# A hybrid decoder step on one core: the mixer's tiles moved under its heads

## What is computed

```python
u = hn @ w_in                       # hn = rmsnorm(h); D_IN = 4640
xa, za, ia, fa, zb, xbc, dtr = split(u)
xc = silu(causal_conv(xa))          # 4 taps
q, k = xc @ w_q, xc @ w_k;  v = xa @ w_v      # per head, 8 heads of 128
h_a = mlstm(q, k, v, ia, fa)        # scores * decay, state C, n, m
h_a = rms(h_a) * norm_a * sigmoid(za)
xs, B, C = split(silu(causal_conv(xbc)))      # 16 heads of 64, state 128, 2 groups
y = ssd(xs, softplus(dtr), B, C) + d_skip * xs
y = group_rms(y * silu(zb)) * norm_b
h = h + concat(h_a, y) @ w_out
h = h + moe(rmsnorm(h))             # 16 experts, top-2 of a top-1 group
```

## Time and profile before

| | us |
|---|---|
| median of 3 runs (lowest, highest) | 933.55 (930.46, 938.48) |
| the profiled execution, its own time | 930.9 |
| its span, first to last instruction | 929.2 |
| PE, DVE, ACT, POOL busy | 830.6, 316.4, 149.8, 104.2 |
| mean granted TensorE clock | 0.955 of full |

### The profile page before, as it was taken

One profiled execution on the slowest core, in us unless ns is written; L12 is line 12 of the kernel. 1 busy time (PEld: TensorE's weight loads), 2 busy tenths in 40 slices (PEclk: granted clock), 3 DMA queues, 4 the chain that ended last, 5 costly groups with the idle time before them and its releaser, 6 DMA issues.

```text
span 929.2 us, 9631 instructions
## 1 busy us (share of the span) xinstructions
PE 830.6 (89%) x3774; PEld 443.0 (48%) x3774; DVE 316.4 (34%) x635; ACT 149.8 (16%) x368; POOL 104.2 (11%) x135
## 2 busy tenths in 40 slices
PE   5999999998587789999999899989899788999785
PEld 4888788665344458875332243322433223333221
DVE  3966601699978740043002012002111020020203
ACT  2222211543211220051110010100000100101002
POOL 5000000574644410000000000000000000000000
PEclk9999999998677779989999999999999999999999
DMA  8834333568565424930799999999999999999992
GB/s 241 269 113 159 134 115 136 159 194 247 155 183 161 130 84 183 358 115 1 303 409 410 409 409 410 409 409 409 409 409 409 409 409 410 409 409 410 409 409 105
DMA packets 110067, 263.01 MB, mean 283 GB/s; under 512 B 7127, under 2 KB 46219, under 8 KB 110009
## 3 DMA queue, kind: packets, MB, share of 16 engines
q1 hardware_dynamic: 107856, 257.94, 74.2%
q0 software_dynamic: 1648, 3.33, 1.2%
q10 hardware_dynamic: 520, 1.15, 0.4%
HBM read 251.66 MB, written 10.91 MB: 283 GB/s over the span
## 4 chain that ended last, share of the span: by engine, by line
PE 60%; DMA 14%; DVE 13%; SPq 8%; issue 2%; ACT 2%; ACTq 0%; DVEq 0%
PE bank L1421 13%; PE bank L1736 13%; DMA ring<-in_w_up 10%; PE bank L1788 8%; SPq L557 8%; PE bank L1638 6%; PE bank L1718 6%; DVE shared L1090 4%; PE bank L1751 3%; DMA ring<-in_w_down 2%; PE bank L1603 2%; DVE ring L1114 2%; DVE h_tok L1109 2%; PE bank L1560 1%; DVE YS L1118 1%
## 5 line engine op out<-in xcount | busy, mean ns | idle before, releaser
L1736 PE MATMUL bank<-ring,arena 128*64 128x512 f32 x1024 | 226.8, 594 | 26.4 <-DMA ring<-in_w_up 20.1
L1736 PEld LDWEIGHTS bank<-ring,arena 128*64 128x64 f32 x1024 | 73.3, 137 | 176.9 <-issue 131.6
L1421 PE MATMUL bank<-arena,ring 128*128 128x280 f32 x576 | 136.2, 399 | 0.8 <-ACT arena L797 0.8
L1788 PE MATMUL bank<-ring,arena 128*64 128x512 f32 x512 | 113.6, 595 | 14.6 <-ACT arena L942 14.2
L1421 PEld LDWEIGHTS bank<-arena,ring 128*128 128x128 f32 x576 | 109.4, 190 | 27.6 <-issue 1.2
L1355 DVE TENSOR_TENSOR arena<-bank,arena 128x512 f32<-128x512 f32 x16 | 11.1, 692 | 244.2 <-PE bank L1736 244.2
L1788 PEld LDWEIGHTS bank<-ring,arena 128*64 128x64 f32 x512 | 36.4, 137 | 81.6 <-issue 78.9
L1638 PE MATMUL bank<-arena,ring 128*128 128x264 f32 x256 | 59.6, 394 | 0.0
L434 DVE COPY arena<-bank 64x512 f32<-64x512 f32 x16 | 10.9, 683 | 137.9 <-PE bank L1788 137.9
L1718 PE MATMUL bank<-arena,xn 128*128 128x256 f32 (+1 forms) x192 | 54.2, 412 | 0.7 <-DVE arena L1327 0.7
L1638 PEld LDWEIGHTS bank<-arena,ring 128*128 128x128 f32 x256 | 49.5, 195 | 9.3 <-issue 0.7
(11 more groups left out here) (336 smaller groups left out, 749.2 us busy)
## 6 DMA issues: line engine op xcount, KB each, us to landing
ring<-in_w_gate SPq DMA_DIRECT2D x32, 2048.0 KB, 21.1
ring<-in_w_up SPq DMA_DIRECT2D x32, 2048.0 KB, 23.5
ring<-in_w_down SPq DMA_DIRECT2D x32, 2048.0 KB, 19.8
ring<-in_w_in SPq DMA_DIRECT2D x9, 2048.0 KB, 8.7
ring<-in_w_out SPq DMA_DIRECT2D x4, 2048.0 KB, 8.0
out<-h_tok SPq DMA_DIRECT2D x16, 512.0 KB, 3.5
h_tok<-in_state_ssm SPq DMA_DIRECT2D x8, 512.0 KB, 5.2
h_tok<-in_state_mlstm_C SPq DMA_DIRECT2D x8, 512.0 KB, 5.2
```

Source lines behind the costliest of these rows:

```text
L1421: last = mm(bank[n % 4][:, 0:T], slot_k(u % MR, 512)[:, k, o:o + P], hT[:, k, :], start=(k == 0), stop=(k == KD - 1))
L1736: last = mm(b[CAP * half:CAP * (half + 1), :], XG[:, k, e * CAP:(e + 1) * CAP], w[:, kk, half * 512:(half + 1) * 512], start=(k == 0), sto ...
L1788: last = mm(bank[5][CAP * half:CAP * (half + 1), :], HT[:, kk, u * CAP:(u + 1) * CAP], w[:, kk, half * 512:(half + 1) * 512], start=(u == ...
```

## The change

The mixer is put in another order, the arithmetic is the same up to rounding and these identities: silu(y) = (tanh(y/2) + 1) * y/2, with conv weights and biases halved beforehand (V_CAW to V_NB and from V_CBB); sigmoid likewise; 1/sqrt by Sqrt and a VectorE reciprocal in place of Ln and Exp.

- TensorE: after the 8 xa tiles and the tables the mLSTM heads begin. The x/B/C tiles stand inside them, two in each of heads 0 to 3, one in each of heads 4 to 7; the z tiles, zb first, stand ahead of the SSD heads, one each. All these 28 tiles use one PSUM bank, 5 (`b5_free`). The output projection begins before the last scales are done, and has no scales stage ahead of it: heads' scales are broadcast inside the SSD heads and inside the projection.
- The C states go by head and not by sample: a block holds one head's C of all 8 samples; it is decayed, updated and read in that head. The read is eight calls with a single weight column, one per sample, to partitions 0, 32, 64, 96 of banks 0 and 1, summed by two more calls. The SSD states go into the SSD heads, one sample in two heads.
- V of the samples goes to DRAM and back per head (`v_rows`).
- The decay products of the states and XWT move from GpSimd to ScalarE (eight, or six, activations with a scale by partition); the first convolution step, with the bias, moves from VectorE to ScalarE; the k of the samples is copied and weighted by VectorE. GpSimd only issues DMAs and copies a column per head.
- The scores of SSD heads are multiplied straight from PSUM (`GT` is gone).
- Weight blocks: order xa, qkv, x/B/C, zb, za, w_out, with an explicit list of slots. The first three expert blocks are requested before the last w_out block.

The core of the diff:

```diff
-WIN = [O_XA, O_XA + 512, O_XBC, O_XBC + 512, O_XBC + 1024, O_ZA, O_ZA + 512, O_ZB, O_ZB + 512]
-U_QKV = len(WIN)
+WIN = [O_XA, O_XA + 512, None, O_XBC, O_XBC + 512, O_XBC + 1024, O_ZB, O_ZB + 512, O_ZA, O_ZA + 512]
+U_QKV = WIN.index(None)
...
+UNIT_SLOT = [0, 1, 2, 0, 1, 0, 1, 2, 0, 1, 2, 0, 1, 2]
...
+XBC_A, XBC_B = [0, 2, 4, 6, 8, 9, 10, 11], [1, 3, 5, 7]
```

On SP:

```diff
+            def v_rows(h):
+
+                sp.wait_ge(s.v_sb, h + 1)
+                sp.dma_start(v_dram[h].rearrange("(b e) -> b e", e=P), VS[:, h * P:(h + 1) * P]).then_inc(s.rows_out, 16)
+                sp.wait_ge(s.rows_out, 32 + 16 * (h + 1))
+                if h >= 2:
+                    sp.wait_ge(s.st_new, h - 1)
+                sp.dma_start(VB[h % 2], v_dram[h:h + 1, :].to_broadcast([P, NB * DH])).then_inc(vb_in[h % 2], 16)
...
+            v_rows(0)
+            for h in range(HA):
+                row_load(h + 4)
+                if h + 1 < HA:
+                    v_rows(h + 1)
+                state_step(h)
...
+            expert_unit(0, 0, s.y_ps, HB)
+            expert_unit(0, 1, s.yb_norm, KD)
+            expert_unit(0, 2, s.yb_norm, KD)
+            mixer_unit(U_OUT + 3)
```

On ScalarE:

```diff
+            def decay_state(n):
+
+                act.wait_ge(st_in[n % 3], 16 * (n // 3 + 1))
...
+                for j in range(NB):
+                    w = BCM[:, n, j:j + 1] if n < HA else XE[:, j, n - HA:n - HA + 1]
+                    part = state_buf(n)[:, j, :]
+                    last = a.activation(part, part, ACT.Copy, scale=w)
+                last.then_inc(s.st_dec, 1)
...
+            for h in range(HA):
+                first_tap(3 + 2 * h)
+                first_tap(4 + 2 * h)
+                tanh_of_conv(2 + 2 * h)
                 if h + 1 < HA:
                     head_in(h + 1)
+                decay_exp(h + 1)
+                tanh_of_conv(3 + 2 * h)
+                decay_state(h + 1)
+                evac(HA + XBC_A[h])
...
+                cq_copy(h)
                 head_out(h)
+                if h < 4:
+                    evac(HA + XBC_B[h])
+                if h == 4:
+                    lct_copy(2, bank[5], s.b5_free)
...
+            for h in range(HB):
+                if h + 1 < HB:
+                    decay_exp(HA + h + 1)
+                if h % 2 == 0:
+                    weighted_x(h // 2)
+                elif h + 1 < HB:
+                    decay_state(HA + h // 2 + 1)
+                z_tanh(h)
+                if h % 2 == 0 and h >= 2:
+                    y_square(h // 2 - 1)
+                if h == 3:
+                    a.preload_act_table(ACT.Sqrt)
```

On VectorE, in the mLSTM heads:

```diff
+                c_update(h)
+                conv_taps(3 + 2 * h)
+                if h + 1 < HA:
+                    sample_q_k(h + 1)
+                conv_gate(2 + 2 * h)
+                conv_taps(4 + 2 * h)
+                conv_gate(3 + 2 * h)
```

On VectorE, in the SSD heads:

```diff
+                c = h // 2
+                dve.wait_ge(s.gt_ps, h // (HB // NG) + 1)
+                weighted(HA + h, bank[3 + h // (HB // NG)])
                 if h + 1 < HB:
                     ssd_args(h + 1)
+                if h == 1:
+                    denominators()
+                if h == 4:
+                    head_scales()
                 if h % 2 == 0 and h >= 2:
+                    ssd_out(dve, c - 1)
+                    gate_y(c - 1)
+                    s_read(c - 1)
+                if h % 2 == 1:
+                    s_update(c)
+                if h < KD:
+                    dve.wait_ge(s.z_sig, h + 1)
+                    v.scalar_tensor_tensor(out=ZB[:, h, :], in0=ZB[:, h, :], scalar=1.0, in1=bank[5][:, 0:T],
+                                           op0=ALU.add, op1=ALU.mult).then_inc(s.b5_free, 1)
+                if h % 2 == 1 and h >= 9:
+                    num_out((h - 9) // 2)
```

On TensorE:

```diff
+            def c_read(h):
+
+                pe.wait_ge(s.st_new, h + 1)
...
+                for b in range(NB):
+                    j = b % 4
+                    last = mm(bank[b // 4][32 * j:32 * j + 1, QT:QT + P], QS[:, h, b:b + 1], state_buf(h)[:, b, :],
+                              start=True, stop=True, skip_group_check=True)
+                last.then_inc(s.cq_ps, 1)
...
                 if h + 1 < HA:
                     head_proj(h + 1)
+                if h >= 1:
+                    squares_sum(h - 1)
+                xbc_tile(XBC_A[h])
+                c_read(h)
                 pe.wait_ge(s.st_done, h + 1)
...
+                if h < 4:
+                    xbc_tile(XBC_B[h])
+                elif h == 4:
+                    pe.wait_ge(s.b5_free, B5_LCT)
+                    lc_rows(2, bank[5])
+                else:
+                    pe.wait_ge(s.b5_free, B5_XS[h - 5])
+                    xs_rows(h - 5, 0, bank[5])
...
             for h in range(HB):
                 c = h // 2
+                if h >= 1:
+                    z_tile(h)
...
+            out_unit(0)
+            pe.wait_ge(s.b5_free, B5_Z + 2 * KD)
+            pe.wait_ge(s.st_done, HA + HB)
+            out_parts(range(4), (5, 4))
+            head_rows(4)
```

899 lines of the change are left out of this document (476 added, 423 removed).

## The result

| | before | after |
|---|---|---|
| median of 4 runs (lowest, highest), us | 934.75 (930.46, 938.48) | 893.12 (886.08, 893.72) |
| ratio, with its 95% interval | | 0.9539 (0.9475 to 0.9603) |
| profiled execution, its span, us | 930.9, 929.2 | 893.4, 891.7 |
| mean granted TensorE clock | 0.955 | 0.983 |

The kernel became 4.6% faster; 892 had been forecast. Twelve more runs of the changed kernel, beside the experiments, gave 884.3 to 894.1.

A forecast was written before the change was run, and what follows sets the result against it. The end was taken as the first expert matmul plus 487 us, bound by expert weights. Stages sum to 341.7 against 383.5 us, 41.8 earlier: span 887.4, and with offsets of 1.7 and 2.65, 892 us; range 873 to 920.

The forecast's parts named there:

- first expert matmul plus 487: Whole kernel: the end comes 487 us after the first expert matmul, whatever the mixer does, with expert weights streaming at 409 GB/s.
- mLSTM heads: Eight heads with x/B/C tiles: TensorE's work sets the period, 17.1 us in heads 0 to 3, 14.0 after; 124.4 in all.
- TensorE-bound already: mLSTM heads of the kernel before: TensorE already sets the period of a head, 7.42 us.
- v through DRAM: V's write and load per head: hidden in heads 1 to 7, a TensorE stall of 3.1 us in head 0.
- Hand-over: Between mLSTM and SSD heads: transposes, one z tile, sums and products take 13.2 us, VectorE's last convolutions ending under the transposes.
- from 50 us to the router except at head 0: Sign expected in the profile after: TensorE's granted clock is full over this whole stretch.
- SSD heads: Sixteen heads with z tiles: 11.8 us a pair, plus 5 for two stretches with reciprocals queued ahead; 96.2 in all.
- Output projection: After the SSD heads: 61.6 us as before plus 4.0 for broadcasts and sums, 65.6; last scales and last w_out block hidden.
- (1), in-order waits: Fixed-order ScalarE and VectorE queues delay 28 tiles 0.7 us each, C read unhalved: 919 us, or 905 at half; chance 0.27.
- (2), bank 5's hand-over: Evacuation behind a state decay costs each of 28 tiles 3.0 us: 976 us; chance 0.10 for anything past 924.
- (3), the tables: ScalarE alternates tanh and exp tables, 48 loads of 1.28 us, hidden under mLSTM heads, 24 us in SSD heads: 916; chance 0.04.
- (4), C reads four at once and head 0's wait covered: These and the reciprocals' stalls covered give 880 us, down to 873 if the tables' stretch shrinks; chance 0.12.

The follow-up runs named there:

- all three moves: Changed kernel with last mLSTM head's C copy before two tanh, z's first tanh before the DMA waits, reciprocals after gate products: 884.94 us; again 888.15.
- repetition (1): The changed kernel run once more with nothing altered, as control of its group: 892.57 us, ratio 0.9591.
- repetition (2): The changed kernel run once more with nothing altered, as base on its companions' chip: 889.91 us, ratio 0.9559.

## Why the prediction was right

The sum of the stages, by its own terms; measured is the profiled execution of after. (The terms of the hand-over as printed in the prediction add up to 13.3, not 13.2; nothing hangs on it.)

| term | predicted | measured |
|---|---|---|
| xa tiles | 30.4 | 30.2 |
| tables | 5.7 | 6.2 |
| first head projection | 3.1 | 4.7 |
| mLSTM heads, with head 0's wait | 127.5 | 115.8 |
| hand-over | 13.2 | 17.4 |
| SSD heads | 96.2 | 103.7 |
| output projection | 65.6 | 65.6 |
| sum | 341.7 | 343.6 |

To this come 4.3 us in the start (25.8 instead of 21.5), which belong to this execution and not to the change (two repetitions start at 21.3 and 21.7), and -2.0 in router and gathering. Span 887.4 was predicted, 891.7 measured; the median fell on the forecast because it lies 0.3 below the profiled execution here and not 2.65 above it as taken. The result is right to 1 us, and that is luck in the size, though not in the mechanism (TensorE's own calls set the periods of the heads and the tiles hide the rest): the mLSTM heads were 11.7 too long in the sum, hand-over and SSD heads 11.7 too short.

*What bounds the kernel, "first expert matmul plus 487".* Held: 37.7 us earlier (404.3 for 442.0), 487.4 after it. Not quite "whatever the mixer does": in four of twelve traces the stage took 490.0, because its first matmuls ran at a lower clock.

*mLSTM heads.* Right that TensorE's sum sets the period and that the decays are hidden. Over-counted: head 7 projects nothing for a next head, and its 3.1 us had been counted twice; so had the last C sum and squares (1.2), which stand in the hand-over's sum too; the wait of 3.1 in head 0 didn't come; the C read cost 0.54 and not 0.9 (2.9 us over eight heads), its sum 0.36 and not 0.6 (1.9), and squares 0.55 for 0.61 (0.5). The experiment with one strip shows why: 1.84 us without strips, 0.54 with four, 3.4 times as fast; I had taken half, from halves of PSUM in the earlier trace rows. Against it, a tile between other calls takes 3.97 ahead of a C read and 3.88 ahead of a C sum, not 3.80: 0.08 to 0.17 each, of the order of the 0.15 a switch that was weighed in the prediction and not put into the sum. One premise was too strong: that a head of the kernel before is "TensorE-bound already". Its eight heads took 64.0 us, 8.0 each, against the 7.42 of the one read; with the decays off GpSimd they took 2 us less. The Trainium skill, "TensorE: Matmul & The Clock Gate", Part 3, gives 2.38 times for three column tiles, which was nearer to this than my half; the four strips measured here give more than that, and agree in direction.

*v through DRAM.* Not the 3.1 us of wait. The chain has the write at 67.67 (1.20 us), the load at 68.89 (3.53) and VectorE's update from 72.49 to 74.68; TensorE reached the C read at 75.0. All of this lies 6.4 us later than in the sum, and so does TensorE's want (68.6 + 6.4), but the round trip was 4.7 us and not 6.8, since the write took 1.20 and not the 3.45 taken from another path. The update came 3.4 us earlier than the sum has it, so 1.3 of that are not accounted for. A wait of 0.69 remained ahead of the next tile.

*Hand-over.* 4.2 too short. A wait that I had not seen (2.7, the copy of the last C read behind two tanh) and the lower clock after it. The experiment with that copy first shows both: 14.3 instead of 17.8, near the 13.2 of the sum. The full clock that the prediction expected "from 50 us to the router except at head 0" was missing here and behind the waits of the SSD heads.

*SSD heads.* 7.5 too short. Three waits, 7.7 us together: 4.25 for a DMA that ScalarE waits for ahead of z's first tanh, which the sum had not; 1.41 behind the chain of denominators, in which VectorE itself waits 1.62 us for a sum of TensorE; and 2.08 behind the second reciprocal, so 3.5 where 5 had been taken. Behind the waits stand three tiles of 5.73, 5.1 us more than at the full clock, that the sum had not either: this is the larger part of the 7.5, since the sum had 7.4 us of waiting as well (5 for the reciprocals and 0.3 in each of eight pairs for bank 5, which did not come), only in other places. The experiments show them: with the tanh first 97.2, with all three moves and the clock at 1.00 94.4, under the 96.2 of the sum. Steady pairs took 11.5 (heads 6 and 7) and 12.1 (from head 8 on, with the broadcasts), 11.8 in the mean, as taken: no wait for bank 5, but 0.08 to 0.17 more a tile.

*Output projection.* Exact to 0.1, scales and last w_out block hidden.

**The rivals.** (1), in-order waits: right in kind (the waits found are of this kind), small in size, 10.4 us of waiting in four places and not 0.7 on each of 28 tiles. (2), bank 5's hand-over: not here; in the block of z tiles it costs 0.5 to 1.0 us a tile, so it is the work between the tiles that hides it, as the prediction argued. (3), the tables: none between tanh and exponential; the two loads inside the SSD heads (at 226.5 and 228.4 us) are those put there for the Sqrt. With Sigmoid there are 48 more, the number of the rival, at about 9 us and not 24: an exponential wanted a head ahead has time, so most loads lie off the path. So the replacement of Sigmoid isn't what makes the interleaving "possible at all", as the prediction has it: with Sigmoid the kernel still takes 3.4% less than before. The Trainium skill, "ScalarE: Activation LUTs", Table sets, puts tanh in exp's set; the trace agrees, with no load between the two in 36 tanh. (4), C reads four at once and head 0's wait covered: both came, and were spent in the hand-over and at the z tiles.

**What the gain is made of.** The parts don't add. The decays moved alone give 18 of the 42 us in the old order; undone alone in the new one they cost nothing that can be measured. Moving them relieves VectorE beside GpSimd's products, and with z tiles under the heads VectorE has 104 us for 75 to 81 us of work instead of 80 for 64. That either measure covers the same shortage is my reading of these figures; it wasn't tried by itself. The z tiles as a block lose 50, more than the whole gain, and about 39 without the waits for the one bank, nearly the whole. So the interleaving carries the result; tanh for Sigmoid is worth about 9 us of it, and the strips some 7 net by the stages of one trace. How much of the gain the x/B/C tiles under the mLSTM heads bring by themselves was not tried.

## What to carry to other kernels

Where TensorE runs short of work in one stage and is the bound in another, add up one period by TensorE's own calls and lay the independent tiles under the short stage; a single bank then suffices, if each tile has other matmuls behind it, and doesn't if it has none. Before trusting such a sum, walk the other engines' queues at the seams between stages: the steady periods came out within 0.8 us of the sum, and 7 of the 10 us of waits stood at seams, behind a wait written for something else (a DMA's source buffer, a tanh of another stream). When a part is credited, try it both alone and undone: here one part was worth 18 us in one order and nothing in the other.

## What the runs showed of the hardware

A wait of TensorE costs more than its length. After waits of 1.4 to 4.4 us a tile of 16 instructions often took 5.73 us for 4.04 (7.09 once), at a reduced granted clock (0.80 over a hand-over of 17 us); two waits of 1.4 and 0.5 in place of one of 2.7 left it at 1.00 in three traces of three. The same wait (1.41 in two traces of the same kernel) was followed by a slow tile in one and by a fast one in the other, this in the repetition (1), so the clock isn't a function of the wait alone:

```profile
209.43 4.04 PE L1529 MATMUL bank<-arena,ring 128*128 128x280 f32 x16 [1.41 <-DVE arena L1297]
```

Such a piece at the lower clock costs 1.7 us in most places where it can be read by itself: the tiles (5.73 for 4.04) and the first 64 matmuls of the experts (15.65 for 13.95). With the start below, these pieces make up most of the spread between traces of one kernel.

The same program starts in two ways. The sixteen calls of the gate columns in after and in its repetition (1), lines of the instructions at L1506:

```profile
L1506 PE MATMUL bank<-arena,WG x16: 399/674/755, 19.0 to 25.4; 128*80 128x280 f32 x16
```

```profile
L1506 PE MATMUL bank<-arena,WG x16: 399/399/463, 17.5 to 21.1; 128*80 128x280 f32 x16
```

674 ns median against 399, with the granted clock shown as 1.00 in both. It comes with 1.5 us more in the tables and the first head, 5.8 us together, which is most of the distance between runs near 885 and near 893; the rest are slow gate tiles, as the repetition (2) shows, with the early start and a span of 888.2. What decides the start stays open.

Eight reads with one weight column each, to four strips of PSUM, took 0.54 us where the same eight to one strip took 1.84.
